# VectorE's expert stage unrolled, and the choice of experts spread between the dot products

## The reference

```python
q = (xc @ peer_wq).reshape(TOKEN_CHUNK, PEER_HEADS, PEER_DQ)
s1 = einsum('chd,nd->chn', q[..., :half], peer_keys[0]);  s2 = ...   # 128 keys each
v1, i1 = lax.top_k(s1, 16);  v2, i2 = lax.top_k(s2, 16)
cand_s = v1[..., :, None] + v2[..., None, :]                         # 256 candidates
top_s, pos = lax.top_k(cand_s, 16)
e = cand_i at pos                                                    # 16 of 16384 experts
g = softmax(top_s)
h = gelu(einsum('cd,chkd->chk', xc, peer_u[e]))
out = einsum('chk,chkd->cd', g * h, peer_v[e])
```

## Time and profile before

| | before |
|---|---|
| timed runs, median | 1257.37 us |
| profiled execution, span | 1367.7 us |
| PE busy | 1084.5 us (79%) |
| POOL busy | 893.1 us (65%) |
| DVE busy | 707.6 us (52%) |
| ACT busy | 419.0 us (31%) |
| DMA, mean over the span | 261 GB/s |

### The profile page before, as it was taken

The page is one execution under the profiler, slowest core; times in us unless marked ns, Lnnn a source line. Parts: engine busy times, 40 slices in busy tenths (PEclk is TensorE's granted clock), DMA queues, the critical chain, the costliest instruction groups (busy, mean ns, idle before and its releaser), DMA issues.

```text
span 1367.7 us, 14268 instructions
## 1 busy us (share of the span) xinstructions
PE 1084.5 (79%) x4842; PEld 736.2 (54%) x4842; DVE 707.6 (52%) x1601; ACT 419.0 (31%) x761; POOL 893.1 (65%) x845
## 2 busy tenths in 40 slices
PE   6999999999999989996858657855965676586557
PEld 5778897999988868893313223322322232232222
DVE  5336233111444874694656637636547636744842
ACT  4345454444436443633202211220121022102202
POOL 6765457888896683686566667667476557557670
PEclk9999999999999989998978778778987888798778
DMA  6443325455453402599899999999798899889891
GB/s 250 158 150 108 109 87 191 161 179 180 176 196 141 152 3 93 175 384 357 312 384 351 349 389 366 351 354 399 270 405 317 331 365 367 326 336 402 333 410 66
DMA packets 89442, 356.86 MB, mean 261 GB/s; under 512 B 9648, under 2 KB 9776, under 8 KB 81840
## 3 DMA queue, kind: packets, MB, share of 16 engines
q0 software_dynamic: 73728, 268.47, 50.7%
q1 hardware_dynamic: 15232, 86.15, 17.6%
q10 hardware_dynamic: 432, 1.57, 0.3%
HBM read 355.10 MB, written 1.05 MB: 260 GB/s over the span
## 4 chain that ended last, share of the span: by engine, by line
DVE 22%; issue 10%; another core or an unknown queue 9%; PE 4%; POOL 4%; DMA 1%; DVEq 1%; ACT 0%; POOLq 0%; ACTq 0%
DVE u_row L1903 14%; PE bank L1009 4%; POOL u_row L2026 2%; POOL v_row L2026 2%; DMA v_row<-peer_v_dram,expert 1%; DVE gain L1833 1%; DVE gain L1882 1%; DVE c_part L1885 1%; DVE gain L1884 1%; DVE gain L1874 1%; DVE s_idx L1836 1%; DVE s_idx L1840 1%; DVE c_top L1830 1%; DVEq L1387 0%
## 5 line engine op out<-in xcount | busy, mean ns | idle before, releaser
L1009 PE MATMUL bank<-v_row,diag 128*128 128x512 f32 x960 | 483.0, 655 | 226.6 <-issue 191.3
L1988 POOL TENSOR_TENSOR w_lo<-raw,w_hi 128x512 fp32r<-128x512 f32 x296 | 375.0, 1300 | 161.4 <-ACT w_hi L1127 161.0
L1009 PEld LDWEIGHTS bank<-v_row,diag 128*128 128x128 f32 x960 | 199.5, 210 | 509.7 <-issue 475.3
L2026 POOL DMA_INDIRECT u_row<-peer_u_dram,expert x256 | 248.9, 972 | 151.9 <-issue 72.2
L1903 DVE CUSTOM_DVE_ANT_0 u_row<-u_row,bank 128x1024 f32<-128x1024 f32 x256 | 295.5, 1217 | 28.1 <-issue 17.1
L2026 POOL DMA_INDIRECT v_row<-peer_v_dram,expert x240 | 225.1, 938 | 111.5 <-issue 69.3
L610 PE MATMUL bank<-hT_hi,w_hi 128*128 128x256 f32 x672 | 193.2, 287 | 7.0 <-issue 3.7
L611 PE MATMUL bank<-hT_lo,w_hi 128*128 128x256 f32 x672 | 191.5, 285 | 3.3 <-issue 3.1
L612 PE MATMUL bank<-hT_hi,w_lo 128*128 128x256 f32 x672 | 191.7, 285 | 2.5 <-issue 2.5
L1127 ACT ACTIVATE w_hi<-raw 128x2048 fp32r<-128x2048 f32 x79 | 150.7, 1910 | 109.1 <-PE bank L612 64.7
L1348 ACT ACTIVATE gelu<-dots 128x16 f32<-128x16 f32 x16 | 3.5, 216 | 462.2 <-issue 274.4
(11 more groups left out here) (260 smaller groups left out, 1340.8 us busy)
## 6 DMA issues: line engine op xcount, KB each, us to landing
raw<-stream_dram SPq DMA_DIRECT2D x79, 1024.0 KB
u_row<-peer_u_dram,expert POOLq DMA_INDIRECT x256
v_row<-peer_v_dram,expert POOLq DMA_INDIRECT x240
residual<-x_in_dram SPq DMA_DIRECT2D x2, 512.0 KB, 4.5
out_dram<-residual SPq DMA_DIRECT2D x4, 256.0 KB, 2.1
consts<-consts_in_dram SPq DMA_DIRECT2D x1, 840.0 KB, 13.1
gain<-norm_final_dram ACTq DMA_DIRECT2D x1, 512.0 KB, 6.0
normed_tokens<-norm_g_dram ACTq DMA_DIRECT2D x1, 512.0 KB, 3.6
```

The costliest lines, as they stand in the source:

```text
L1009: ins = mm(accs[half][:, :], diag[:, 2 * m + i, :], row[:, half * 512:(half + 1) * 512], start=False, stop=True, skip_group_check=True)
L1988: ins = nc.gpsimd.tensor_tensor(w_lo[r][:, cols], raw[r][:, cols], w_hi[r][:, cols].bitcast(F32), ALU.subtract)
L2026: nc.gpsimd.indirect_dma_start(rows[2 * m + i][:, :], None, table_in, bass.IndirectOffsetOnAxis(ap=expert[:, b, 2 * m + i:2 * m + i + 1], ...
```

## The change

Only VectorE's program changes.
- The loop over groups 2 to 13 is written out; every wait of VectorE on its own steps is on a constant.
- `choice(n)` is `choose` as a generator with 13 steps. It reads `match` where it lies, without the copy to `s_work`. Each step ends in an increment (`last_of_step`), and the wait for it stands later.
- `group(g)` now chooses the experts of group g+2, not g+1: it waits until the key scores of group g+2 are there (`match_done`), issues step 1, and then after each of the 16 dot products waits for the last step and issues the next one. So the 13 steps stand ahead of row 0 and behind rows 0 to 11. After `weights(g)` it writes the expert numbers of g+2 (`name_experts`).
- The wait for `v_free` ahead of the choice is gone. Instead `name_experts(n)` waits, for n from 3 on, until the v rows of group n-3 have all landed (`v_in`), as it overwrites their indices.
- Group 0 and group 1 take the same form. The choice of group 2 moves from the middle of group 1 to group 0; the last split stands behind row 3 of group 0 as before.

```diff
-                if in_loop[0]:
-                    dve.wait_ge(dve_step, loop_step)
-                    dve.reg_add(loop_step, loop_step, 1)
-                else:
-                    dve.wait_ge(dve_step, steps[0])
+                dve.wait_ge(dve_step, steps[0])
...
-            def choose(g, b):
-
-                both = match[:, :, :].rearrange("p g n -> p (g n)")[:, bass.ds(g * 2 * NKEY, 2 * NKEY)]
-                settle(v.tensor_copy(s_work[:, 0, :, :].rearrange("p w n -> p (w n)"), both))
...
+            def choice(n):
+
+                b = n % 3
+                lists = [(match[:, n, w * NKEY:(w + 1) * NKEY], s_top[:, w, :], s_work[:, 1, w, :], s_idx[:, w, :]) for w in range(2)]
...
+                for values, top, left, index in lists:
+                    ins = v.max(top[:, 0:8], values)
+                yield step_done(ins)
+                for values, top, left, index in lists:
+                    ins = v.match_replace(left, top[:, 0:8], values, TAKEN)
+                yield step_done(ins)
...
+            def name_experts(n):
+
+                b = n % 3
+                if n >= 3:
+                    dve.wait_ge(v_in[BATCHES - 1], (n - 2) * PAIR_IN)
                 v.scalar_tensor_tensor(expert[:, b, :], c_part[:, 0, :], float(NKEY), c_part[:, 1, :], ALU.mult,
                                        ALU.add).then_inc(experts_ready, 1)
...
-            def group(g, b, more=True):
-
-                if more:
-
-                    dve.wait_ge(v_free, g * BATCHES - BATCHES)
-                    choose(g + 1, (b + 1) % 3)
-                dot_products(g, range(BATCHES))
-                weights(g, b)
...
+            def group(g):
+
+                chosen = g + 2 < TT * NH
+                if chosen:
+                    dve.wait_ge(match_done, g + 3 if g + 2 < NH - 1 else TT * NH)
+                    todo = choice(g + 2)
+                    done = next(todo)
+                for row in range(ETOP):
+                    dot_product(g, row)
+                    if g == 0 and row == 3:
+                        late_split(NGRAN - 1)
+                    if chosen and done is not None:
+                        dve.wait_ge(dve_step, done)
+                        done = next(todo, None)
+                weights(g)
+                if chosen:
+                    name_experts(g + 2)
...
+            for g in range(TT * NH):
+                if g == NH:
+                    settle(v.tensor_copy(hn_tile[:, :], hn[:, 1, :]))
+                group(g)
```

## The result

| | kernel before | changed kernel |
|---|---|---|
| median of 20 runs | 1256.57 us | 1263.64 us |
| span of the profiled execution | 1367.7 us | 1261.6 us (device time 1263.39 us) |

Ratio 1.006, 95% interval 1.0038 to 1.0082: the change makes the kernel slower by 5 to 10 us. The profile of before stands 110 us above its timed runs, that of after agrees with its own. The prediction took the 110 us for an effect of profiling; the experiments show that it isn't.

The account below looks back on a forecast made before the run. The prediction took DMA at full rate, 410 GB/s, to bound timed runs. To 1257.4 us it added 4.3 us for group 0, all else 0: 1261.7 us, forecast's own range 1260 to 1264, overall 1251.0 to 1264.0.

Parts of the forecast that it names:

- The group 0 term: Choice steps between group 0's dot products delay GpSimd's u gathers of group 1: 4.3 us idle DMA, bounds 0 and 6.3.
- 2.0 us of queued DMA work: Gathers already queued when GpSimd falls behind in group 0 cover 2.0 us of its 6.3 us delay.
- groups 1 to 13: VectorE needs 27.6 us a group against 40.9 us of DMA, so the change costs 0 there.
- the end: Groups 14, 15 and shared rows, untouched by the change: 0; 10 us allowed for it in a timed run.
- The base of the sum: Timed run before: gathers start at 577 us, 660 us of DMA at 410 GB/s, 10 us of end: 1247 us.
- The 0.7 us steps belong to the profiled execution: VectorE's and TensorE's slow issue after a burst occurs only when profiled; timed runs have DMA at full rate but for 10 us.
- The spaced balance: In the profiled execution alone, the hole at 650 to 660 us goes and stalled choice moves: span 1290 to 1345 us.
- unrolling, constant waits, copy and v_in wait: VectorE's written-out loop, constant waits, dropped match copy and replaced v_free wait: each 0 on the end.
- query early, no wait for it: Last query's weight split moves to 606.3 to 608.5, TensorE needs it at 610.54: 0, with 2.0 us of cover.
- experts of group 2: Named right after group 0's weights: gain 0, or 6.3 us if the trace's order holds; late-experts rival, 1253.5 us, chance 0.25.
- the 2.7 us margin: In timed runs before, group 2's experts are ready at 641.1, 2.7 us ahead of GpSimd's last v gather at 643.8.
- The 425 GB/s of the Trainium skill: Rate for a 16 MB transfer; by it DMA needs 637 us, leaving 33 us of room; prediction kept 410 GB/s.

Follow-up runs that it names:

- j: Changed kernel with 24 more comparisons on VectorE ahead of group 0's dot products; 1.0025 of the kernel before, median 1362.6 us, spaced chip.
- h: Changed kernel, GpSimd issuing a pair of u gathers only after the u pair two before has landed; 0.9897 of the kernel before, median 1345.0 us, spaced chip.
- before_again: Kernel before, unchanged, timed and profiled again on a spaced chip; ratio 1.0002, median 1369.3 us, profiled span 1368.0 us.
- k: Changed kernel, group 2's choice behind group 0's weights, in groups 1 to 13 the whole choice ahead of the dot products; 1.0003 of the kernel before, spaced chip.
- l: Changed kernel with the whole choice as one block behind dot products and weights in groups 0 to 13; 0.9895 of the kernel before, spaced chip.
- c: Changed kernel with group 2's choice as one block behind group 0's weights; 0.9898, 0.9827 and 0.9854 of the kernel before on three spaced chips.
- after_again2: Changed kernel, unchanged, run again on another spaced chip; 0.9840 of the kernel before, span 1338.3 us.
- m: Changed kernel with a 16-column GpSimd write and a wait for it behind every second gather of groups 2 to 15; 1409.6 us, quick chip.

## Why the prediction was right or wrong

- **Direction and size on a quick chip.** Forecast 1261.7 us, +4.3 us; measured 1263.64 us, +7.1 us by the medians and +4.8 to +10.3 us by the interval. Scaled by the ratio, 1257.4 x 1.006 = 1264.9 us lies 0.9 us above the range.
- **The group 0 term** shows in the trace as it was named: GpSimd waiting for dot products, DMA below full rate at 610 to 630 us, and no row behind it in which it is made up. No run takes the steps out on a quick chip, so that they are the cause of the loss is read from the trace. Its size, 4.3 us forecast against 3.9 us of missing transfers, agrees, but by luck: its inputs were off and cancelled. The last u gather of group 1 was put 6.3 us later and came 2.4 us later: between dot products twelve steps cost 6.2 us, not 7.7 (a dot product seems to hide the settling), and group 0 began 1.9 us earlier than in the earlier trace rows. And the 2.0 us of queued DMA work that I subtracted covered nothing that can be seen: the last gather is 2.4 us late and 3.9 us of transfers are missing, and j against h, where it starts at 642.23 instead of 626.61 (15.6 us late), misses 17.9. Why more is missing than the gather is late I can't resolve; the trace of before is from a spaced chip.
- **The failed step is the sum 1257.4 + 4.3**, in which group 0 is the only term and groups 1 to 13 and the end stand at 0. The medians differ by 7.1 us, of which group 0 shows 3.9, also below the interval's lower end of 4.8; some 3 us more are in no row that can be named. In groups 1 to 13 there is no room for them: the rate is 410 GB/s from 660 to 1200 us. At the start of the gathers the changed kernel is no slower either: from 575 to 600 us its five 5 us stretches carry 274, 314, 371, 401 and 418 GB/s, those of before 246, 305, 326, 407 and 418. That leaves the end, which was put at "untouched", and differences of the rate too small for these rows. The uneven end of the 16 DMA engines (1244.4 to 1251.6 us) would be a place: in before, whose engines had pauses, the rate falls from 421 to 60 GB/s within two slices of 0.75 us. Whether the kernel before has such an end on a quick chip isn't known, so the cause of these 3 us stays open.
- **The base of the sum** was off as well. It read 577 + 660 + 10 = 1247 us and left at most 10 us of room for holes. In the changed kernel's trace the start misses 3.5 us (204, 354 and 386 GB/s in the three stretches from 577 to 592), and from the fall of the rate to the span's end it is 17 us, not 10. With these, 577 + 660 + 3.5 + 17 = 1257.5 us of span, and the 3.9 us of group 0 on top give 1261.4, against 1261.6: nothing else is missing in the changed kernel's trace. The kernel before, at 1256.57 us less the 1.8 us around a span, has 1254.8: it leaves no room for holes at all, and is even 2.7 us quicker than its start and end would be if they were the changed kernel's. These are, by this account, the 3 us that stay open.
- **"The 0.7 us steps belong to the profiled execution"** was wrong as a cause, and right as a reason to leave them out of the forecast for the timed runs. They go with the chip: before_again takes 1357 to 1387 us in every timed run. I had a span of 1367.7 and times of 1257.4 and took the profiler for the difference; that the two came from different conditions was not among my rivals.
- **The spaced balance** was forecast for the profile alone, span 1290 to 1345 us. On spaced chips it was 1342.4 and 1338.3 us, inside, though at the slow end, and the reason given (the stalled choice no longer ahead of the dot products) is what k against l and c shows. In the changed kernel's first profile, a quick one, the span was 1261.6 us, outside.
- **Right on the quick chip**: no effect of unrolling, constant waits, copy and v_in wait that the trace shows (VectorE idles 223.5 us for rows); query early, no wait for it; experts of group 2 named at 624.20, long before GpSimd wants them at 646.5, hence no gain. I had them at 641.1 under the *old* order, so the 2.7 us margin itself stays untested.
- **The 425 GB/s of the Trainium skill** ("DMA: Bandwidth & Descriptors", Measured) has no row here either: the page of the changed kernel has 409 to 411 in every full slice, and the fullest 5 us stretch, behind a hole, 420 (after_again2).

No version that ran beats both kernels. c is the candidate: on spaced chips it can't be told from the changed kernel, and on a quick one it should lose nothing; that wasn't measured.

## What to carry to other kernels

When a profiled span and the timed runs differ by more than the few microseconds around the span, ask which chip, and which moment, each came from before calling the difference an artefact; run the unchanged kernel again beside every experiment. On an engine that frees buffers for a saturated queue, put the freeing work first and the preparation behind or between it, except in the first round, where each further microsecond cost one here (j). A saturated resource hides most edits, so look for the stretch where it isn't saturated yet.

## What the hardware showed that I had not expected

- Two conditions of a chip for one kernel: 1257 us on one, 1364 to 1371 us on four. The spaced ones issue an instruction every 0.7 to 4 us after a short burst while the gathers run, on TensorE and VectorE alike; TensorE's idle time put down to issue from 660 to 1200 us is 137.9 us on one (before_again) and 0 in the quick profile. VectorE's loop and a deep DMA queue aren't the cause; what is stays open.
- After some 610 us at full rate the 16 DMA engines seem not to end together: the rate falls to 20 to 31 GB/s, about a sixteenth of 410, and the last rows come 7 us after it began to fall (changed kernel, quick).
- A wait on GpSimd for its own write of 16 columns took 0.86 us before the next gather, which without it follows after 0.30 us (m).
- Twelve steps mixed between 1.14 us dot products cost 6.2 us (after), a fifth less than the 7.7 us in a block (before).
